# The first four weight chunks of the memory's keys, from the attention steps to the row slots

## What is computed

```
# first block
proj = rms_norm(x) @ w_in                # 6 x 512 columns
mq, mk, mv, dq, dk, dv = split(proj)     # 8 plain heads of 64, 4 differential heads of 2 x 64
a_out = causal_attention(mq, mk, mv)     # 8 units, one map each
b_out = (A1 - lam * A2) @ dv             # 4 units, two maps each
x = x + mixed(a_out, b_out) @ w_out
q = rms_norm(x) @ peer_query             # expert choice: 8 heads x 16 experts per token
x = x + sum_e gate_e * gelu(down_e . x) * up_e   # one 8 KB row pair per token and expert
# second block, in its cross attention
k, v = split(rms_norm(mem) @ w_xkv)      # mem: 256 x 1024, keys 1024 and values 1024 columns
```

## Time and profile before

| | us |
|---|---|
| median of 3 runs | 1402.89 |
| lowest and highest | 1401.67, 1402.97 |
| the profiled execution | 1401.84 |
| its span | 1400.0 |
| PE busy | 1250.1 (89%) |
| POOL busy | 887.4 (63%) |
| DVE busy | 812.8 (58%) |
| ACT busy | 612.2 (44%) |

### The profile page before, as it was taken

One profiled execution on the slowest core, in us unless ns is written; L12 is line 12 of the kernel. 1 busy time (PEld: TensorE's weight loads), 2 busy tenths in 40 slices (PEclk: granted clock), 3 DMA queues, 4 the chain that ended last, 5 costly groups with the idle time before them and its releaser, 6 DMA issues.

```text
span 1400.0 us, 17652 instructions
## 1 busy us (share of the span) xinstructions
PE 1250.1 (89%) x5974; PEld 887.6 (63%) x5974; DVE 812.8 (58%) x1575; ACT 612.2 (44%) x1296; POOL 887.4 (63%) x533
## 2 busy tenths in 40 slices
PE   7999999888988987677787898999999999999997
PEld 6878785444444533233333344799999988899886
DVE  5934397777877677877667654603652632277301
ACT  5566434334443442322333323447455345555432
POOL 5633766555766645544544451996868964799985
PEclk9999999999999998899999899999999999999999
DMA  7532489999999999999999996464636633455652
GB/s 264 182 104 75 166 316 389 425 427 425 417 426 426 424 427 426 427 426 428 428 426 419 419 427 273 145 207 133 188 126 201 206 123 121 137 194 182 208 195 92
DMA packets 72943, 400.69 MB, mean 286 GB/s; under 512 B 8096, under 2 KB 8352, under 8 KB 39712
## 3 DMA queue, kind: packets, MB, share of 16 engines
q0 software_dynamic: 36864, 268.45, 45.8%
q1 hardware_dynamic: 33696, 123.35, 27.1%
q10 hardware_dynamic: 2304, 7.85, 1.5%
HBM read 396.48 MB, written 3.15 MB: 285 GB/s over the span
## 4 chain that ended last, share of the span: by engine, by line
PE 35%; DMA 21%; issue 16%; POOL 15%; DVE 7%; ACT 4%; POOLq 0%; ACTq 0%; SPq 0%; DVEq 0%
DMA arena<-in_experts,arena 21%; POOL w_lo L1413 12%; PE bank L896 9%; PE bank L600 8%; PE bank L602 7%; PE bank L601 7%; DVE arena L1778 4%; POOL arena L1464 3%; PE bank L653 1%; ACT arena L1224 1%; ACT diag L1230 1%; DMA ring<-in_stream 1%; PE bank L662 0%; DVE arena L1718 0%; ACT arena L1063 0%
## 5 line engine op out<-in xcount | busy, mean ns | idle before, releaser
L1413 POOL TENSOR_TENSOR w_lo<-ring,w_hi 128x1024 fp32r<-128x1024 f32 x222 | 560.9, 2549 | 183.6 <-ACT w_hi L1050 182.7
L896 PE MATMUL bank<-arena,diag 128*128 128x512 f32 x968 | 459.0, 626 | 90.9 <-ACT diag L1230 90.9
L1464 POOL DMA_INDIRECT arena<-in_experts,arena x242 | 287.0, 1186 | 244.3 <-PE bank L896 184.2
L1778 DVE CUSTOM_DVE_ANT_0 arena<-arena 128x1024 f32<-128x1024 f32 x242 | 318.9, 1331 | 163.5 <-DMA arena<-in_experts,arena 163.3
L896 PEld LDWEIGHTS bank<-arena,diag 128*128 128x128 f32 x968 | 187.0, 199 | 342.4 <-issue 206.7
L1050 ACT ACTIVATE w_hi<-ring 128x1024 fp32r<-128x1024 f32 x228 | 240.0, 1058 | 175.2 <-PE bank L602 121.6
L600 PE MATMUL bank<-hT_hi,w_hi 128*128 128x256 f32 x736 | 210.4, 286 | 5.8 <-DVE hT_lo L1499 2.7
L602 PE MATMUL bank<-hT_hi,w_lo 128*128 128x256 f32 x736 | 206.4, 280 | 0.0
L601 PE MATMUL bank<-hT_lo,w_hi 128*128 128x256 f32 x736 | 206.2, 280 | 0.0
L1221 ACT ACTIVATE arena<-arena 128x2 f32<-128x2 f32 (+2 forms) x99 | 20.2, 204 | 408.5 <-DVE arena L1778 408.3
L600 PEld LDWEIGHTS bank<-hT_hi,w_hi 128*128 128x128 f32 x736 | 139.1, 189 | 11.6 <-issue 10.3
(11 more groups left out here) (251 smaller groups left out, 1673.2 us busy)
## 6 DMA issues: line engine op xcount, KB each, us to landing
ring<-in_stream SPq DMA_DIRECT2D x228, 512.0 KB, 3.6
arena<-in_experts,arena POOLq DMA_INDIRECT x242, 14.7
kv_park<-arena ACTq DMA_DIRECT2D x8, 256.0 KB, 7.7
arena<-kv_park ACTq DMA_DIRECT2D x1, 2048.0 KB, 7.7
x_res<-in_x SPq DMA_DIRECT2D x2, 512.0 KB, 5.4
arena<-in_mem SPq DMA_DIRECT2D x1, 1024.0 KB, 11.4
arena<-in_sub_keys ACTq DMA_DIRECT2D x1, 1024.0 KB, 6.5
out<-arena SPq DMA_DIRECT2D x2, 512.0 KB, 2.6
```

The source lines that it names most:

```text
L896: mm = pe.matmul(y_banks[half][:, :], diag[:, slot % DIAGS, :], rows_buf[BUFFER[slot]][:, D + 512 * half:D + 512 * half + 512], start=(i = ...
L1413: nc.gpsimd.tensor_tensor(w_lo[:, slot, :], ring[:, slot, :], w_hi[:, slot, :].bitcast(F32), ALU.subtract).then_inc(S("lo_made"), 1)
L1464: nc.gpsimd.indirect_dma_start(out=rows_buf[b], out_offset=None, in_=experts, in_offset=bass.IndirectOffsetOnAxis(ap=expert_u[:, slot:slot ...
L1778: v.tensor_tensor_reduce(out=rows_buf[b][:, 0:D], in0=xn[:, slot // (PEER_H * PEER_K), :], in1=rows_buf[b][:, 0:D], scale=1.0, scalar=0.0, ...
```

## The change

All eight key chunks become `xk_late` and go to row slots, so 16 chunks of the memory (8 of values, 8 of keys) stand behind the query chunks, at slots 64 to 124 in place of 64 to 108. `MORE` goes from 119 to 141 and `PAIRS` from 120 to 140. The first four `turn_heads`, the two scores of the first unit and that of the second move in among the last four chunks of `w_in`; ACT copies the last value columns (`values_out(5)`) behind the first exponentials. Every later score gets one `keep_busy`. The transposed probabilities run two steps behind the scores in place of three. The norm of `mem` moves from step 1 to steps 11 and 12, and PE waits for it at the value chunks. `PLAIN_TURNED` goes from 2 to 4. The two early parks and a wait for them ahead of the sub keys' DMA go.

```diff
-CHUNK_AT += [CHUNK_AT[-1] + 9 + 4 * i for i in range(12)]
+CHUNK_AT += [CHUNK_AT[-1] + 9 + 4 * i for i in range(16)]
...
-FEW, MORE, PAIRS, FEWER = 72, 119, 120, 199
+FEW, MORE, PAIRS, FEWER = 72, 141, 140, 199
...
-STREAM = [("w_in", 24), ("xk", 4), ("w_out", 8), ("query", 16), ("xv0", 4), ("xv1", 4), ("xk_late", 4),
+STREAM = [("w_in", 24), ("w_out", 8), ("query", 16), ("xv0", 4), ("xv1", 4), ("xk_late", 8),
...
+            bank = turn % (4 if among else ROPE_BANK if first else 8)
+            if key in EARLY_BANK:
+                bank = EARLY_BANK[key]
             else:
                 turn = bank + 1
         table[key] = ((bank, uses[bank]), chunk, results, last)
...
+    for g, half in TURN_ORDER[:4]:
+        place, chunk, results, _ = table["qkT", g, half]
+        table["qkT", g, half] = (place, chunk, results, LAST["w_in"] - 3)
...
-KEY_PIECES = {step: n for step, n in zip(range(3, 12), (4, 4, 3, 4, 3, 4, 3, 4, 3))}
-KEY_BANK = 6
 TURNED_BY_DVE = (3, 5, 7)
 OUT_CHUNKS = [(0, 2), (0, 3), (1, 2), (1, 3), (0, 0), (0, 1), (1, 0), (1, 1)]
-PLAIN_TURNED = 2
+PLAIN_TURNED = 4
+EARLY_BANK = {("qkT", 2, 0): 1, ("qkT", 3, 0): 2, ("qkT", 0, 0): 3, ("qkT", 1, 0): 5, ("score", 8): 6, ("score", 9): 7}
...
-        mem, memn = tiles(A(22784, 2048)), tiles(A(24832, 2048))
-
-        stage = [A(8192 + 512 * i, 512) for i in range(2)] + [A(7168 + 512 * i, 512) for i in range(2)]
+        mem, memn, mem_junk = tiles(A(22784, 2048)), tiles(A(29440, 2048)), tiles(A(24832, 2048))
+
...
-            for n in range(6):
+            for n in range(5):
                 natural("w_in", 4, n, h_, FIRST["w_in"], normed("attn") if n == 0 else None)
...
-            pe.wait_ge(S("roped"), 4)
-            turn_heads(TURN_ORDER[:4])
...
+            def among_values(i):
+
+                if i == 2:
+                    pe.wait_ge(S("roped"), 4)
+                    turn_heads(TURN_ORDER[:4])
+                elif i == 3:
+                    for m in maps_of(HEAD_ORDER[0]):
+                        score(m)
+
+            natural("w_in", 4, 5, h_, FIRST["w_in"], among_values)
+            for m in maps_of(HEAD_ORDER[1]):
+                score(m)
+
...
-            xk_banks = {}
-
-            def memory(piece):
-
-                i, k = piece // KT, piece % KT
-                c = FIRST["xk"] + i
-                if i % 2 == 0 and k == 0:
-                    xk_banks[i // 2] = open_bank(pe, ("xk", i // 2))
-                if k == 0:
-                    wait_weight(c)
-                mm = product(xk_banks[i // 2][:, i % 2 * T:(i % 2 + 1) * T], weight(c, slice(k * P, (k + 1) * P)),
-                             hT[k], k == 0, k == KT - 1)
-                if k == KT - 1:
-                    mm.then_inc(chunk_done, 1)
-
             for step in range(16):
                 if step == 5:
                     turn_heads(TURN_ORDER[6:])
-                if step < 12:
+                if 2 <= step < 12:
                     for m in maps_of(HEAD_ORDER[step]):
-                        score(m, 4 if step == 0 and m == MAP_ORDER[0] else 0)
+                        score(m, 1)
                 if step == 1:
+                    turn_heads(TURN_ORDER[4:6])
+                if step == 11:
                     norm("mem", memn)
-                    turn_heads(TURN_ORDER[4:6])
-                if step in KEY_PIECES:
-                    if keys_done(step) == 0:
-                        for g in range(4):
-                            normed("mem")(g)
-                    for piece in range(keys_done(step), keys_done(step + 1)):
-                        memory(piece)
-                if 3 <= step < 15:
-                    turn_probs(HEAD_ORDER[step - 3], 2 if step >= 12 else 0)
+                if 2 <= step < 14:
+                    turn_probs(HEAD_ORDER[step - 2], 2 if step >= 12 else 0)
...
+                if i < 4:
+                    normed("mem")(i)
...
+            def values_out(n, t):
+
+                act.wait_ge(S("rstd"), 2 * seq["attn"] + t + 1)
+                copy_out(("w_in", n, t), proj1[n][:, t, :], rstd["attn"][:, t:t + 1])
+
+            for n in range(5):
                 for t in range(TT):
                     hi_before(("w_in", n, t))
                     bank = take(act, ("w_in", n, t))
                     if n < 4:
                         nc.scalar.activation(sq1[n][:, t * 512:(t + 1) * 512], bank[:, :], ACT.Square)\
                           .then_inc(S("squares"), 1)
-                    else:
-                        act.wait_ge(S("rstd"), 2 * seq["attn"] + t + 1)
-                        copy_out(("w_in", n, t), proj1[n][:, t, :], rstd["attn"][:, t:t + 1])
+                    elif n == 4:
+                        values_out(n, t)
...
-                    sumsq("mem", mem, memn)
+                    sumsq("mem", mem, mem_junk)
                 if n == 4:
+                    act.wait_ge(S("roped"), 4)
...
-            for step in range(13):
+            for step in range(14):
                 if step < 12:
                     for m in maps_of(HEAD_ORDER[step]):
                         exps(m)
+                if step == 0:
+                    for t in range(TT):
+                        values_out(5, t)
                 if step == 1:
-                    norm_out("mem", con("g_mem"))
                     heads_out(TURN_ORDER[4:6])
                 if step == 4:
                     heads_out(TURN_ORDER[6:])
-                if step == 6:
-                    park([(("xk", 0), None)], "xk", 0)
-                if step == 9:
+                if step == 10:
                     att_square(range(8, 12), slice(512, 1024))
-                if step >= 1:
-                    u = HEAD_ORDER[step - 1]
+                if step >= 2:
+                    u = HEAD_ORDER[step - 2]
                     if u not in TURNED_BY_DVE:
                         copy_out(("pT", u), pT[:, u, :], n=SC)
-            park([(("xk", 1), None)], "xk", 1)
-            hi_parts(LAST["xk"] + RING)
+                if step == 12:
+                    norm_out("mem", con("g_mem"))
+            hi_parts(LAST["w_in"] + RING)
...
-            act.wait_ge(S("kv_parked"), 16 * 2)
...
+                    if slot == CHUNK_AT[-13] + 3:
+                        park(values(0), "xv", 0)
                     if slot == CHUNK_AT[-9] + 3:
-                        park(values(0), "xv", 0)
-                    if slot == CHUNK_AT[-5] + 3:
-                        act.wait_ge(S("kv_parked"), 16 * 4)
+                        act.wait_ge(S("kv_parked"), 16 * 2)
                         park(values(1), "xv", 1)
-                    if slot - 3 in CHUNK_AT[-3::2]:
-                        n = CHUNK_AT[-3::2].index(slot - 3)
-                        act.wait_ge(S("kv_parked"), 16 * (6 + n))
+                    if slot - 3 in CHUNK_AT[-7::2]:
+                        n = CHUNK_AT[-7::2].index(slot - 3)
+                        act.wait_ge(S("kv_parked"), 16 * (4 + n))
...
-            for step in range(12 + 3):
+            for step in range(12 + 4):
...
-                if step == 1:
-                    norm_low("mem", con("g_mem"))
...
-                if step == 10:
+                if step == 12:
+                    norm_low("mem", con("g_mem"))
+                if step == 11:
...
-                if step == 13:
+                if step == 12:
...
-                if step >= 3:
-                    u = HEAD_ORDER[step - 3]
+                if step >= 4:
+                    u = HEAD_ORDER[step - 4]
```

38 lines of the change are left out of this document (15 added, 23 removed).

## The result

| | before | after |
|---|---|---|
| median, us | 1402.28 (4 runs) | 1428.49 (4 runs) |
| lowest to highest | 1397.01 to 1402.97 | 1425.10 to 1431.58 |
| profiled execution (its span) | 1401.84 (1400.0) | 1425.1 (1423.3) |

The account below looks back on a forecast made before the run. DMA bounds the row slots, PE the attention. Attention gain -7.3, clock +3.3 and slot bytes +6.1 sum to +2.1 us on 1401.84: 1403.9; the median lies 1.05 higher, so 1404.9 us, range 1399.0 to 1409.5.

Parts of the forecast that it names:

- The step that failed: In the row slots, 11 buffers in place of 13 from slot 119 to 141 and twenty more paired slots cost nothing.
- The clock term: In the attention, PE's new waits bring two half-clock stretches of 3.4 us, 3.3 us lost.
- the clock falls and stays down: Rival, attention: light matmuls behind the 3.2 us wait don't raise the clock; 6.6 us lost gives 1408.3 us; chance 0.28.
- for the values: Ahead of attention step 1, PE idles 3.2 us until ACT has written the last value columns.
- the first rival: Attention: the clock stays up through the 13 fillers and short waits; gain 7.3 us, 1401.7 us in all; chance 0.2.
- for the memory norm: Near the attention's end, PE waits 1.8 us for a bank holding a transposed quarter of `mem`.
- for the last probabilities: At the attention's end, DVE's remaining work ahead of the last unit's probabilities makes PE wait 1.7 us more.
- for the plain half: With `PLAIN_TURNED` = 4 the needing chunk stands right behind the plain half's transposes: 1.5 us of PE wait.
- The bytes in the slots: Row slots: four chunks and two parks, 2.62 MB at 427 GB/s, add 6.1 us; bounds 4.9 and 8.1.
- The fillers, 6.2 us: Attention steps 2 to 11: 13 extra matmuls in PE's own queue at 0.48 us each, none hidden, 6.2 us.
- The price of the pairs: Attention: a filler between two maps of one unit takes the pair apart, 0.8 us, up to 2.4.
- the 5.0 us of clock: Attention of the kernel before: two half-clock stretches, 3.5 and 6.7 us long, lose 5.0 us.

Follow-up runs that it names:

- busy_wait: fewer195 with six matmuls whose result nobody reads put into PE's wait for the values ahead of step 1: 1401.97 us, ratio 1.0013.
- wait_later: fewer195 with PE's wait for the values moved from ahead of step 1 to ahead of step 4: 1408.92 us, ratio 1.0047.
- four_chunks_less: The changed kernel with FEWER = 195 and four of the eight key chunks left out, parking writes kept: 1401.43 us.
- fewer195: The changed kernel with FEWER = 195 in place of 199, so the buffer numbering has no step: 1413.86 us, ratio 1.0066.
- fill_waits: values_first with PLAIN_TURNED = 2 and, in place of the 13 fillers, eleven only where PE waits in no_fillers: 1397.44 us, ratio 0.9974.
- no_fillers: values_first with PLAIN_TURNED = 2 and without the 13 fillers ahead of the scores of steps 2 to 11: 1398.69 us, ratio 0.9987.
- values_first: fewer195 with ACT writing the values ahead of the three roundings of the first exponentials: 1403.61 us, ratio 1.0010.

## Why the prediction was wrong

**The step that failed** is the sentence "Fewer buffers from slot 119 to 141 (11 in place of 13) and twenty more slots in pairs cost nothing". It looked at how many buffers there are, and for that it was right: without a step the rate is 424 to 428 GB/s in each stretch of the slots that was read (230 to 500, 560 to 700 and 720 to 740 us). It didn't look at which buffer a slot has. `MORE` stands in the formula of all slots up to 199, so moving it by 22 shifts the numbering by 22 % 13 = 9 at a place 58 slots further on (slot 199 would have buffer 69 % 13 = 4 in place of 0). With a step of four slots the gathers wait for rows in use; that costs 19.7 us (709.0 less 689.3), and 22.7 in the kernel before. No row of the trace of before could show it; a table of each slot's buffer and the distance to its last use would have.

**The clock term** was 3.3 us, two stretches of 3.4 us. In the profiled execution it was right: two stretches of 3.4 us, and a mean of 0.96 over 76.2 us is 3.0. Over the runs it was not. Four of six executions with this attention took 82 to 86 us for the stretch, and filling the wait was worth 7.4 us by the ratios and 11.9 by the medians. So the rival "the clock falls and stays down" held in most of the profiled executions, in the place that it named, behind the wait for the values. Its 6.6 us are near the 7.4; but I made them of four short stretches, where it is one of 20.5 us that comes or doesn't, and a second, at the end, of nothing to 10 us. Against the 73.4 us of busy_wait the six executions lost 3, 3, 9, 11, 12 and 12 us. The price of a stretch was also the lower of two that the earlier trace rows shows: 1.7 us behind the first wait, 3.3 behind the second. Four times the higher is 13 us, about what the worst executions lost. "The fillers keep it up", the ground for the first rival, was wrong: 13 fillers spread over the steps didn't help where PE stood still 3 us ahead of the first of them. The Trainium skill ("TensorE: Matmul & The Clock Gate", A second HAM failure mode: psum-queue depth-cycling) says that short idle times between groups of matmuls can make the clock swing; the runs agree, as two waits of 1.29 and 2.00 us brought it to 0.66 in wait_later.

**What held.** The waits, forecast and measured: for the values 3.2 and 3.09, for the memory norm 1.8 and 1.70, for the last probabilities 1.7 and 1.40, for the plain half 1.5 and 1.56. The first gather: 4 and 3.7 us earlier. The bytes in the slots: 6.1 and 5.4 (689.3 less 683.9), and 5.9 for 2.1 MB in four_chunks_less, between the bounds of 4.9 and 8.1. With the step removed and the clock held (busy_wait), the time is 1401.97, near the first rival's 1401.7. That nearness is luck in part: the runs of the kernel before that belong to busy_wait have a median of 1400.72, so it is 1.3 us slower than before (1.8 by the ratio), where that rival had it 1.2 us faster.

**What was mis-sized.** The fillers, 6.2 us, "none is hidden": without them 1.7 us were gained at the median, and 3.5 us of longer waits took their place in the profiled execution, since some of them stood where PE would wait anyway. The price of the pairs that were taken apart (0.8) I can't tell from these runs, as no run changed it alone. And the 5.0 us of clock that "come back" from the kernel before are 4.7 in one execution and 3.0 in another, and filling both waits gained 1.2 in the median.

**The parts don't add to the median.** The stages of the profiled executions sum to +23.3 us, the medians differ by 26.2; 1.9 of the 23.3 are in the last stage, which the change leaves alone and which took 531.6 to 537.1 us in these kernels.

## What to carry to other kernels

Where buffers are numbered by a remainder, a moved limit shifts every slot behind it: write down for each slot the distance to the last use of its buffer, before and after, and look for the smallest; where consumers work in batches, a distance near the batch's length drains the pipeline. A wait of an engine whose clock depends on being busy is priced twice, by itself and by what follows at half clock, so fill it with idle work when it can't be removed. In these runs such work in every step gained nothing over such work in the waits alone. A profile is one execution: a term that rests on the clock needs several runs before it is called a gain.

## What the runs showed of the hardware

- Six matmuls of no use, 2.9 us in a wait of 3.1, made the kernel 7.4 us faster by the ratios (11.9 by the medians, of which one lies in the upper of two groups of runs). I had expected fillers to cost their time.
- The same instructions took 76.1 to 85.7 us, the granted clock being what differed, and the spread of the runs is wide where the profile shows long stretches at half clock: 11.2 us in fewer195, against 4.4 in busy_wait and 4.9 in fill_waits. That is no rule: wait_later has 3.4 in five runs, with 0.66 from 88 to 108 us. The Trainium skill ("TensorE: Matmul & The Clock Gate", What's actually happening) says that how many matmuls run slow at a kernel's start varies from run to run; these traces show the same for falls in mid-kernel (3.4 or 20.5 us behind the same wait).
- With waits of 1.15 and 3.39 us at its beginning, a stretch at half clock lasted 34 us, though PE was busy 16.00 of 16.00 us in the second half of it (no_fillers, one execution). With the waits filled the clock stayed full over seven steps of light matmuls (fill_waits, one execution). And with waits of 1.70 and 1.40 us it stayed full in busy_wait and fill_waits, while it fell to 0.50 at the 1.70 us wait in values_first.
- The gathers and the stream together drew 427 GB/s over 140 us. The Trainium skill ("DMA: Bandwidth & Descriptors", Where 436 GB/s comes from) gives about 358 GB/s per core, a memory stack's rate shared by two cores, as what binds transfers from HBM; in these runs, on one core, the measured rate is higher, and the measurement decides.
